# Second block, front stage: the compressed keys' eviction moves ahead of a GELU and a weight split on ScalarE, and VectorE's half of that split moves behind the gated MLP

## The reference, cut to what matters

```python
z = rms_norm(h, pre_mix_g[i]) @ w_in[i]
zq, zkc, zvc, zks, zvs, zkw, zvw, zg, zu, zv = jnp.split(z, split_at, axis=-1)
kc = compress(kv(zkc), ...)          # h = gelu(flat @ w1 + b1); return h @ w2 + b2
vc = compress(kv(zvc), ...)
kc = rope_partial(kc, cmp_pos)
gates = jax.nn.sigmoid(zg...)
...
s_c = einsum(q, kc) * scale          # scores against the compressed keys
p_c = masked_softmax(s_c, ...)
...
mlp = gelu(zu) * (ws @ layer_norm(gelu(zv)) + b_s)
```

## Time and profile before

| | |
|---|---|
| median of three runs | 2528.34 us (2526.78 to 2530.46) |
| time of the profiled execution | 2526.62 us |
| span of that execution in the profile | 2524.8 us |
| TensorE busy | 2298.5 us, 91% of the span |
| VectorE busy | 1464.4 us, 58% |
| ScalarE busy | 1081.1 us, 43% |
| mean granted TensorE clock | 0.955 of full speed |

### The profile page before, as it was taken

The page is one execution under the profiler, slowest core; times in us unless marked ns, Lnnn a source line. Parts: engine busy times, 40 slices in busy tenths (PEclk is TensorE's granted clock), DMA queues, the critical chain, the costliest instruction groups (busy, mean ns, idle before and its releaser), DMA issues. The chain is left out here.

```text
span 2524.8 us, 35857 instructions
## 1 busy us (share of the span) xinstructions
PE 2298.5 (91%) x15154; PEld 1879.3 (74%) x15154; DVE 1464.4 (58%) x2198; ACT 1081.1 (43%) x1709; POOL 260.1 (10%) x146
## 2 busy tenths in 40 slices
PE   5999889789999967998889999997998889999996
PEld 3988667678888855776588888866876688888865
DVE  2133573649778763456677666355466676666353
ACT  3121472557667553245534333243235534333242
POOL 0000101523223210101010000011101010000011
PEclk7999999899999979999989999999999989999998
DMA  8111006212111102230112222312230012222311
GB/s 347 60 51 67 34 1 229 89 50 60 51 51 51 52 26 106 102 115 18 46 67 85 99 100 100 106 53 100 101 117 1 18 67 100 90 94 100 109 66 69
DMA packets 35200, 205.18 MB, mean 81 GB/s; under 512 B 3936, under 2 KB 5472, under 8 KB 14816
## 3 DMA queue, kind: packets, MB, share of 16 engines
q1 hardware_dynamic: 35040, 202.88, 22.8%
HBM read 200.77 MB, written 2.10 MB: 80 GB/s over the span
## 5 line engine op out<-in xcount | busy, mean ns | idle before, releaser
L278 PE MATMUL ps<-a_high,w_high 128*128 128x512 f32 (+1 forms) x1680 | 632.4, 376 | 35.6 <-DVE a_low L2390 22.7
L279 PE MATMUL ps<-a_low,w_high 128*128 128x512 f32 (+1 forms) x1680 | 621.5, 370 | 0.0
L280 PE MATMUL ps<-a_high,w_low 128*128 128x512 f32 (+1 forms) x1680 | 620.9, 370 | 0.0
L278 PEld LDWEIGHTS ps<-a_high,w_high 128*128 128x128 f32 x1680 | 320.6, 191 | 100.5 <-DVE w_low L2004 19.6
L2004 DVE TENSOR_TENSOR w_low<-raw_ring,w_high 128x2048 fp32r<-128x2048 f32 x102 | 234.0, 2294 | 269.7 <-ACT w_high L1998 265.0
L279 PEld LDWEIGHTS ps<-a_low,w_high 128*128 128x128 f32 x1680 | 321.2, 191 | 54.1 <-issue 2.5
L280 PEld LDWEIGHTS ps<-a_high,w_low 128*128 128x128 f32 x1680 | 321.0, 191 | 52.3
L1998 ACT ACTIVATE w_high<-raw_ring 128x2048 fp32r<-128x2048 f32 x102 | 195.3, 1914 | 365.3 <-PE ps L280 279.4
L278 PE MATMUL ps<-x_high,place_high 128*128 128x512 f32 (+1 forms) x720 | 261.3, 363 | 13.0 <-POOL place_low L270 7.9
L279 PE MATMUL ps<-x_low,place_high 128*128 128x512 f32 (+1 forms) x720 | 255.7, 355 | 0.0
L280 PE MATMUL ps<-x_high,place_low 128*128 128x512 f32 (+1 forms) x720 | 255.5, 355 | 0.0
(11 more groups left out here) (372 smaller groups left out, 4002.3 us busy)
## 6 DMA issues: line engine op xcount, KB each, us to landing
raw_ring<-w_dram SPq DMA_DIRECT2D x112, 1024.0 KB, 4.9
arena<-w_dram SPq DMA_DIRECT2D x24, 1024.0 KB, 8.3
place_raw<-wc_dram SPq DMA_DIRECT2D x48, 512.0 KB, 3.6
place_raw<-w_dram SPq DMA_DIRECT2D x11, 1024.0 KB, 4.9
ab_raw<-w_dram SPq DMA_DIRECT2D x10, 1024.0 KB, 5.0
x<-xT_dram SPq DMA_DIRECT2D x4, 512.0 KB, 14.2
out_dram<-x SPq DMA_DIRECT2D x1, 2048.0 KB, 7.2
arena<-r_dram SPq DMA_DIRECT2D x2, 992.0 KB, 7.3
```

The lines of the kernel that those rows point to most:

```text
L278: nc.tensor.matmul(out, wh, xh, start=start, stop=False)
L279: nc.tensor.matmul(out, wh, xl, start=False, stop=False)
L280: return nc.tensor.matmul(out, wl, xh, start=False, stop=stop)
```

## The change

In `stage_front` of both layers, two things are put elsewhere. On ScalarE the wait for `mixed` and the eviction of the keys move ahead of the GELU of `zu1` and of the high half of unit 13. On VectorE the low half of unit 13 moves from ahead of the eviction of `w2` to behind both steps of the gated MLP, ahead of the softmax of `cmp`. No instruction is added or taken away, and the programs of TensorE, GpSimd and SyncE are the same.

```diff
                         last.then_inc(S.act_out, 1)
+                        act.wait_ge(S.mixed, 1)
+                        nc.scalar.activation(kcT, pair("w2")[:, 0, 0:64], A.Identity, bias=vec2("b2k"))\
+                            .then_inc(S.keys, 1)
                         act.wait_ge(S.dve_out, emptied("zu1")[1])
                         nc.scalar.activation(zu[:, 2:4, :], zu[:, 2:4, :], A.Gelu_apprx_tanh).then_inc(S.absolute, 1)
                         stream2.split_high(act, base + 13)
-                        act.wait_ge(S.mixed, 1)
-                        nc.scalar.activation(kcT, pair("w2")[:, 0, 0:64], A.Identity, bias=vec2("b2k"))\
-                            .then_inc(S.keys, 1)
                         act.wait_ge(S.dve_out, emptied("cmp")[1])
@@
                         scaled("zu1", zu[:, 2:4, :])
-                        split_low(dve, base + 13)
                         finished("w2")
@@
                         mlp(0)
                         mlp(1)
+                        split_low(dve, base + 13)
                         finished("cmp")
```

## The result

The change makes the kernel faster. Its median is 2514.65 us (2510.37 to 2515.11, 4 runs) beside 2528.81 us for the kernel before on the same chip (4 runs); the ratio is 0.9941, with a 95% interval of 0.9923 to 0.9958. A second set of runs gave 0.9938 (0.9923 to 0.9953). Taken from the 2528.34 us of before, the first ratio is 2513.4 us and a gain of 14.9 us, the second 15.7 us. The forecast was 2517.3 us and a gain of 11.0, with a range from 2514.0 to 2521.5: right in direction and too small, with 2513.4 just under the low end. As gains, the two intervals reach from 10.6 to 19.5 us and from 11.9 to 19.5 us.

A forecast was written before the change was run, and what follows sets the result against it. TensorE, busy for 91% of the span, was taken as the bound. Gains of 3.4 + 1.8 us (first layer) and 3.7 + 2.1 (second), 11.0 in all, took the median 2528.34 to 2517.3 us; range 2514 to 2521.5.

The forecast's parts named there:

- The wait at L2165: TensorE's wait for ScalarE's key eviction would go, starting `mlp0` 3.42 us earlier in the first layer, 3.68 in the second.
- The clock: Half clock behind the wait would go with it, shortening L2254 by 1.8 us in the first layer, 2.1 in the second.
- The wait of 0.5 us for L2453: TensorE's first-layer wait inside L2254 for the emptying of the `w2` pair, counted within the 1.8 us, would go.
- ScalarE's table load with 0.1 us to spare: GELU's 1.28 us table load, now behind the key eviction, would still end before GELU's data and cost nothing.
- VectorE's cover of 2.9 us: VectorE's softmax would end 2.9 us before TensorE's transposes need it, so the later split of unit 13 costs nothing.
- All that follows in the front stage, and the stages behind, move with it as a whole: Everything after the touched stretch would only start earlier, adding nothing to the 11.0 us gain.
- The rival on the attention stages: The two shifted attention stages would meet a lower clock and lose more than the 11 us gained; chance 0.03.
- The low end of the range: 2514 us, a gain of 14, if attention's clock came out better by one hundredth in both layers.
- the prediction's own price: One hundredth of the clock costs about 1.3 us in an attention stage, taken from two equal stages at 0.95 and 0.96.

The follow-up runs named there:

- fill_dve: `dve_only` with TensorE's wait for the keys filled with 27 matmuls into an unused PSUM bank; ratio 0.9966 to the kernel before.
- dve_only: The kernel before with only the low half of unit 13 moved behind the gated MLP on VectorE, keys still evicted last; ratio 1.0000.
- cover: The changed kernel with VectorE's subtraction for unit 13 made three times in place of once; ratio 0.9941 to the kernel before.
- act_only: The kernel before with only ScalarE's eviction of the keys moved first, VectorE's order unchanged; ratio 0.9996.
- mid: The changed kernel with the keys' eviction between the GELU and the high half of unit 13; ratio 0.9972 to the kernel before.

## Why the prediction came out as it did

**The wait at L2165** (3.42 and 3.68 us): right; counted from the start of `w2`, `mlp0` starts 3.46 and 3.71 us earlier. L2165 starts before L2239's last result is out, and `mlp0` waits 0.17 us for L2375.

**The clock** (1.8 and 2.1 us): right, and now shown by `fill_dve`, which took the idle time away and left the lateness. Sum of the two terms: 5.2 and 5.8 us forecast, 5.32 and 5.86 measured. The wait of 0.5 us for L2453 was worth less than it lasts: without it, in `dve_only`, the stretch of the first layer is 0.2 us shorter.

**ScalarE's table load with 0.1 us to spare**: it had 0.18.

**VectorE's cover of 2.9 us**: 2.95, and `cover` showed both what it hides and what it does not.

**The weight of the two parts.** The sum was right for both together, but its account gave VectorE's part 0.5 us of the first layer and ScalarE's the rest. `act_only` shows that this split means nothing: without VectorE's part the mix of `mlp1` waits 4.34 us for L2453.

**The step that failed** is the sentence "All that follows in the front stage, and the stages behind, move with it as a whole". They did not: the four parts behind, put at nothing, took 5.3 us less. With the 11.2 us in front that makes 16.5 us, against 14.9 and 15.7 by the two ratios. The rival on the attention stages named the mechanism, but priced it as a loss only, at 0.03, and left the tails out, where 3.3 of the 5.3 us lie. The low end of the range gave it one hundredth of the clock in each attention stage, 2.6 us by the prediction's own price. The price came from a misread of the earlier trace rows: the first window reached 1.7 us into the tail, and cut at the right instructions the two equal stages are 3.0 us apart (90.4 and 93.4) and not 1.3. No price for a hundredth of the clock holds either, since 90.9 us were taken at 0.98 and 90.4 at 0.96. The 3 us between equal stages was the size to take for the range, on both sides. The one trace before did not show which way the parts behind would move.

The Trainium skill, TensorE: Matmul & The Clock Gate (What's actually happening), was weighed twice. It says that the clock falls after an idle stretch. The traces agree for waits of 3.63 and 4.34 us; across the 1.83 us of `mid` the clock stayed at 1.00. It calls the point at which the clock changes "run-variable". The time up to `w2` fits that, 1126.7 to 1134.4 us in twelve executions of the same instructions. Behind `w2`, though, the two profiled executions of the changed kernel agreed to 0.05 us in every part, while in those of the kernel before the two attention stages changed places.

## What to carry to other kernels

Where TensorE waits for a small result, look at what stands ahead of its eviction, on each engine that TensorE needs before its next long job. Two such queues may each hide the other, and then half a change measures as nothing. The wait of 3.63 us on TensorE cost its own length and 1.65 and 2.6 us more in clock, and filling it recovered only the clock.

When a change moves the stages behind it in time, allow a few us on both sides for the clock in work that was never touched, and read the touched stretch in the trace: it agreed to 0.01 us between two executions of the changed kernel, and to 0.25 us in the kernel before, where half clock lies in it.

## What the hardware showed that was not expected

- The clock's share in untouched stages: equal attention stages took 90.2 to 93.4 us over twelve profiled executions, and the tail of the first layer 627.7 to 630.3.
- In `act_only` 32 matmuls took 1.97 us ahead of a wait of 4.34 us, and 32 of the same shape 3.68 us behind it.
- A wait of 1.83 us in an otherwise busy stretch did not lower the clock in either layer.
- Half clock early in the attention stage was nearly free: TensorE waited for ScalarE behind it, 1.91 us in place of 3.27.
